# Adaptive sums over the partitions as one 512-column product with ones, columns picked by VectorE, and chunk 2 requested before the rows

## The reference

```python
cond = jax.nn.silu(c)                                   # 1 x 1024
for l in range(DEPTH):                                  # DEPTH = 2
    mod = cond @ ada_w[l] + ada_b[l]                    # ada_w[l]: 1024 x 9216
    sh1, sc1, g1, sh2, sc2, g2, sh3, sc3, g3 = jnp.split(mod, N_MOD, axis=-1)
    hn = _modulate(_rms_norm(h, norm_g[l, 0]), sh1, sc1)
    h = h + 0.5 * g1[:, None, :] * _swiglu(hn, ffn1_w_in[l], ffn1_w_out[l])
    hn = _modulate(_rms_norm(h, norm_g[l, 1]), sh2, sc2)
    h = h + g2[:, None, :] * (mixers(hn @ w_in[l]) @ w_out[l])      # four mixers, in short
    hn = _modulate(_rms_norm(h, norm_g[l, 2]), sh3, sc3)
    h = h + 0.5 * g3[:, None, :] * _swiglu(hn, ffn2_w_in[l], ffn2_w_out[l])
```

## Time and profile before

| | |
|---|---|
| median of 3 runs | 2152.02 us (2151.99 to 2154.15) |
| the profiled execution | 2152.88 us, of which span 2151.1 us |
| TensorE busy | 2051.2 us, 95% |
| VectorE busy | 930.2 us, 43% |
| ScalarE busy | 917.4 us, 43% |
| GpSimd busy | 1332.5 us, 62% |
| mean granted clock of TensorE | 0.974 |

### The profile page before, as it was taken

The page is one execution under the profiler, slowest core; times in us unless marked ns, Lnnn a source line. Parts: engine busy times, 40 slices in busy tenths (PEclk is TensorE's granted clock), DMA queues, the critical chain, the costliest instruction groups (busy, mean ns, idle before and its releaser), DMA issues.

```text
span 2151.1 us, 36602 instructions
## 1 busy us (share of the span) xinstructions
PE 2051.2 (95%) x15510; PEld 1966.5 (91%) x15510; DVE 930.2 (43%) x1761; ACT 917.4 (43%) x1393; POOL 1332.5 (62%) x612
## 2 busy tenths in 40 slices
PE   7999997999989999889999999999999999999998
PEld 4999996899989998769998999989999999988998
DVE  4554776561455477754124422144233432134223
ACT  2443454334444335434444354514544345514543
POOL 1778660477967786217887765505896765405885
PEclk8999998999989999999999999999999999999999
DMA  9997550785689775227555543335554543335552
GB/s 326 357 332 253 186 161 20 254 289 176 195 275 349 244 245 167 79 84 250 177 162 170 170 146 116 103 126 166 186 194 134 192 143 113 118 118 168 185 196 79
DMA packets 356787, 398.18 MB, mean 185 GB/s; under 512 B 8984, under 2 KB 318992, under 8 KB 356624
## 3 DMA queue, kind: packets, MB, share of 16 engines
q1 hardware_dynamic: 356464, 395.65, 55.5%
q10 hardware_dynamic: 160, 0.20, 0.0%
HBM read 394.77 MB, written 1.05 MB: 184 GB/s over the span
## 4 chain that ended last, share of the span: by engine, by line
PE 90%; DVE 5%; ACT 3%; SPq 1%; issue 1%; DMA 1%; DVEq 0%; ACTq 0%
PE bank L706 73%; PE bank L783 5%; PE bank L1108 3%; PE bank L938 1%; PE bank L805 1%; PE bank L900 1%; PE bank L1072 1%; SPq L534 1%; DVE arena L1641 1%; ACT arena L1270 1%; PE bank L697 1%; PE bank L999 1%; DVE arena L1685 1%; DMA arena<-in_ada_w 1%; PE bank L939 1%
## 5 line engine op out<-in xcount | busy, mean ns | idle before, releaser
L672 POOL TENSOR_TENSOR w_lo<-ring,w_hi 128x1024 fp32r<-128x1024 f32 (+2 forms) x608 | 1332.3, 2217 | 798.7 <-ACT w_hi L1169 798.1
L706 PE MATMUL bank<-hn,w_hi 128*128 128x256 f32 x2912 | 848.4, 291 | 26.4 <-DVE hn_lo L1578 15.8
L706 PE MATMUL bank<-hn_lo,w_hi 128*128 128x256 f32 x2912 | 832.4, 286 | 0.0
L706 PE MATMUL bank<-hn,w_lo 128*128 128x256 f32 x2912 | 832.1, 286 | 0.0
L1169 ACT ACTIVATE w_hi<-ring 128x1024 fp32r<-128x1024 f32 (+2 forms) x608 | 576.4, 975 | 485.6 <-PE bank L706 356.8
L706 PEld LDWEIGHTS bank<-hn,w_hi 128*128 128x128 f32 x2912 | 567.6, 195 | 36.7 <-issue 34.6
L706 PEld LDWEIGHTS bank<-hn_lo,w_hi 128*128 128x128 f32 x2912 | 567.8, 195 | 4.5 <-issue 3.8
L706 PEld LDWEIGHTS bank<-hn,w_lo 128*128 128x128 f32 x2912 | 567.3, 195 | 0.0
L706 PE MATMUL bank<-gated,w_hi 128*128 128x256 f32 x1408 | 249.7, 280 | 0.0
L706 PEld LDWEIGHTS bank<-gated,w_hi 128*128 128x128 f32 x1408 | 215.0, 187 | 0.0
L706 PE MATMUL bank<-gated,w_lo 128*128 128x256 f32 x704 | 196.4, 279 | 0.0
(11 more groups left out here) (188 smaller groups left out, 2130.1 us busy)
## 6 DMA issues: line engine op xcount, KB each, us to landing
ring<-in_ffn_w_in SPq DMA_DIRECT2D x88, 1024.0 KB, 6.1
ring<-in_w_in SPq DMA_DIRECT2D x72, 1024.0 KB, 5.1
arena<-in_ada_w SPq DMA_DIRECT2D x35, 2048.0 KB, 10.3
ring<-in_w_up SPq DMA_DIRECT2D x32, 1024.0 KB, 5.4
ring<-in_w_down SPq DMA_DIRECT2D x32, 1024.0 KB, 5.0
ring<-in_ffn_w_out SPq DMA_DIRECT2D x32, 768.0 KB, 4.4
ring<-in_ffn_w_out SPq DMA_DIRECT2D x32, 640.0 KB, 4.0
ring<-in_w_in SPq DMA_DIRECT2D x16, 512.0 KB, 3.6
```

The lines of the kernel that those rows point to most:

```text
L672: pool.tensor_tensor(w_lo[:, q, ks], ring[:, r, k0:k0 + n], w_hi[:, q, ks], ALU.subtract) \
L706: last = mm(out, a, b, start=start and i == 0, stop=stop and i == 2)
```

## The change

1. `ada_reduce` becomes one product: weights are ones (128 x 128), the moving operand is the whole of `ada_acc` (512 columns), the result 128 x 512 in bank 7, the same sums on each partition. From the second one on it first waits until VectorE has taken the columns of the one before it (`ada_taken`).
2. VectorE picks the columns: `take_columns` multiplies 128 x 128 of the bank by the identity and sums each row, four times per chunk, into the new SBUF tile `ada_cols`. `take_sums(n)` does this for all sums up to n that aren't taken yet, after it has waited for their products. `ada_sum` calls it for the sum before its own, `modulation` for all that it needs; `modulation` then adds `ada_cols` instead of PSUM to the bias.
3. Chunks 1 and 3 of layer 0: the product takes one column of `cond` broadcast to 128 weight columns, so its result is on all partitions too; VectorE picks its columns from bank 1. ScalarE's `copy_row` and TensorE's `ada_turn` go. The product of chunk 3 waits until the columns of chunk 1 are taken from bank 1.
4. The request of chunk 2 stands right behind those of chunks 0 and 1, ahead of the rows.

```diff
+ADA_SUMMED = [c for layer in range(L) for c in range(ADA_CHUNKS) if (layer, c) not in ((0, 1), (0, 3))]
...
+        ada_cols = sb("ada_cols", MOD_TILES + 4 * ADA_FIRST)
...
-            for c in range(2):
+            for c in range(3):
                 sp.dma_start(first_ada[c], ada_source(0, c)).then_inc(first_ada_in[c], 16)
...
-            sp.dma_start(first_ada[2], ada_source(0, 2)).then_inc(first_ada_in[2], 16)
...
-                            sp.wait_ge(tensor_done, eng.at("first ada row 3"))
+                            sp.wait_ge(tensor_done, eng.at("first ada 3"))
...
-                n, col = ada_sums(layer, c), ada_column(c)
+                n = ada_sums(layer, c)
                 pe.wait_ge(ada_summed, n + 1)
-                for j in range(4):
-                    js = slice(j * P, (j + 1) * P)
-                    last = mm(bank[:, 7, col + j:col + j + 1], ada_acc[:, n % 2, js], ones[:, 0:1], start=True, stop=True)
-                last.then_inc(ada_reduced, 1)
+                if n:
+                    pe.wait_ge(ada_taken, n)
+                mm(bank[:, 7], ones, ada_acc[:, n % 2], start=True, stop=True).then_inc(ada_reduced, 1)
...
-                        last = mm(bank[0:1, 1, :], cond[:, k:k + 1], first_ada[i][:, j], start=(k == 0), stop=(k == KT - 1))
+                        last = mm(bank[:, 1], cond[:, k:k + 1].to_broadcast([P, P]), first_ada[i][:, j], start=(k == 0),
+                                  stop=(k == KT - 1))
...
-            ada_turn(1)
             ada_reduce(0, 0)
+            pe.wait_ge(vector_done, eng.at("first ada 1 taken"))
             ada_product(3, ((3, 4), (4, 4)))
             ada_reduce(0, 2)
-            ada_turn(3)
...
-            copy_row(1)
             round_chunk("f1in", 0)
-            copy_row(3)
...
+            def take_columns(b, c, done, mark=None):
+                for j in range(4):
+                    js = slice(j * P, (j + 1) * P)
+                    i = dve.tensor_tensor_reduce(out=bank[:, b, js], in0=bank[:, b, js], in1=ident, scale=1.0, scalar=0.0,
+                                                 op0=ALU.mult, op1=ALU.add, accum_out=col(ada_cols, ada_column(c) + j))
+                    if j < 3:
+                        i.then_inc(vector_done, eng.step())
+                    elif done is ada_taken:
+                        i.then_inc(ada_taken, 1)
+                    else:
+                        i.then_inc(vector_done, eng.step(mark))
+
+            taken = [0]
+
+            def take_sums(n):
+                for i in range(taken[0], n + 1):
+                    dve.wait_ge(ada_reduced, i + 1)
+                    dve.sem_inc(passed[1], 1)
+                    take_columns(7, ADA_SUMMED[i], ada_taken)
+                taken[0] = max(taken[0], n + 1)
+
             def ada_sum(layer, c):
+                if ada_sums(layer, c) > 0:
+                    take_sums(ada_sums(layer, c) - 1)
...
                 if summed == (0, 3):
-                    dve.wait_ge(ada_reduced, 2)
                     dve.wait_ge(tensor_done, eng.at("first ada 3"))
+                    take_columns(1, 3, vector_done)
+                    take_sums(1)
                 else:
-                    dve.wait_ge(ada_reduced, ada_sums(*summed) + 1)
+                    take_sums(ada_sums(*summed))
+                dve.wait_ge(vector_done, eng.at())
+                dve.wait_ge(ada_taken, taken[0])
                 at_ = MOD_TILES if first == 0 else first
-                tt(mod[:, first:last], bank[:, 7, at_:at_ + last - first], par_all[:, layer, first:last], ALU.add) \
+                tt(mod[:, first:last], ada_cols[:, at_:at_ + last - first], par_all[:, layer, first:last], ALU.add) \
...
+            dve.wait_ge(tensor_done, eng.at("first ada 1"))
+            take_columns(1, 1, vector_done, "first ada 1 taken")
+            take_sums(0)
             dve.wait_ge(first_ada_in[2], 16)
             partial_sum(1, first_ada[2], bank[:, 3])
```

More of the change, by code:

```diff
@@ L432, in build @@
                      ring[:, 3].rearrange("p (k a) n -> p k (a n)", a=2))
-        ada_row = act_tmp[0:1]
         gated = rounded("gated", 8192, FT, 2, S)
@@ L487, in build @@
         first_ada_in = [sem(f"first_ada_in_{i}") for i in range(5)]
-        ada_summed, ada_reduced = sem("ada_summed"), sem("ada_reduced")
+        ada_summed, ada_reduced, ada_taken = sem("ada_summed"), sem("ada_reduced"), sem("ada_taken")
         x_in, tables_in, rows_in = sem("x_in"), sem("tables_in"), sem("rows_in")
@@ L826, in ada_product @@
                     for j in range(nk):
-                        last = mm(bank[0:1, 1, :], cond[:, k:k + 1], first_ada[i][:, j], start=(k == 0), stop=(k == KT - 1))
+                        last = mm(bank[:, 1], cond[:, k:k + 1].to_broadcast([P, P]), first_ada[i][:, j], start=(k == 0),
+                                  stop=(k == KT - 1))
                         k += 1
-                last.then_inc(tensor_done, eng.step(f"first ada row {c}"))
-            def ada_turn(c):
-                pe.wait_ge(scalar_done, eng.at(f"ada row {c}"))
-                col = ada_column(c)
-                for j in range(4):
-                    last = mm(bank[:, 7, col + j:col + j + 1], ada_row[:, c // 2, j * P:(j + 1) * P], ones[0:1, 0:1],
-                              start=True, stop=True)
                 last.then_inc(tensor_done, eng.step(f"first ada {c}"))
@@ L1297, in attention @@
                     after(i)
-            def copy_row(c):
-                act.wait_ge(tensor_done, eng.at(f"first ada row {c}"))
-                f(ada_row[:, c // 2], bank[0:1, 1, :], ACT.Copy).then_inc(scalar_done, eng.step(f"ada row {c}"))
             norm_root("f1")
-            copy_row(1)
             round_chunk("f1in", 0)
-            copy_row(3)
             for layer in eng.layers("one"):
```

## The result

The changed kernel takes **2160.83 us** (median of 5 runs, 2159.46 to 2162.86), the kernel before 2151.99 in the same comparison (2151.27 to 2154.15). The ratio is 1.004, 95% interval 1.0028 to 1.0052: slower by 8.8 us between the medians, 6 to 11 by the interval. The forecast was 2155.0 with a range of 2148 to 2163, and gave slower by over 0.2% a chance of 0.43, no difference 0.50. The profiled execution took 2160.83 with a span of 2159.0, against 2152.88 and 2151.1: +7.95 us to explain where the prediction had +2.95.

A forecast was written before the change was run, and what follows sets the result against it. TensorE, 90% of the chain, was taken as the bound. Stalls 4.95 and boundaries 0.9, less 0.9 for reductions and 2.0 at the start, gave +2.95 us on 2152.88; less 0.86 for the median, 2155.0, range 2148 to 2163.

The forecast's parts named there:

- likeliest case: Whole kernel: the start's gain and the stalls nearly cancel; 2155 us, own range 2151 to 2160, chance 0.52.
- rival 2: Feed-forward loop: the wait costs more, with no slack anything added counts about 11 times; 2163 us, chance 0.24.
- the loop: f1in and f2in: reduction, picks, sum, multiplication, rounding, GpSimd's split, then TensorE's product of the next pair but one.
- the stall: f1in and f2in: TensorE waits for GpSimd's split at every second pair, 0.3 us each; 2.4 us in f1in.
- the picks: VectorE, between reduction and sum: four picks of 0.21 us, 0.84 in all, plus a 0.13 gap.
- TensorE's own part: Reductions in the matmul stream: one wide product plus the pair's matmuls takes 0.03 us less per sum, -0.9 us in all.
- stalls at each pair: Feed-forward loop: a listed sign of being wrong, since stalls were expected only at every second pair.
- f2in: Second feed-forward's 'in' stage: layer 0 two stalls, 0.6 us, plus 1.65 at pair 5; layer 1 one stall, 0.3.
- The stretched add: Modulation's add, f2in pair 3, layer 0: slowed beside GpSimd's split, +1.5 us for the sum, 1.65 us of stall.
- the boundary: Before norm z: VectorE picks a whole chunk, 0.95 us less slack; +0.7 in layer 0, +0.2 in layer 1.
- the start: Early chunk 2 request: chunk 3 lands 1.0 us earlier, its product regains 1.0 of clock loss; -2.0 us.
- rival 5: Start: the early request brings nothing, since the rows' requests are pushed back by as much; 2157 us, chance 0.08.

The follow-up runs named there:

- e2: The changed kernel with the feed-forward 'in' stages' picks moved from ahead of the pair's sum to behind its last gating; 2153.01 us, 1.0001 to the kernel before.
- e5: The changed kernel with each pick that stands ahead of a sum done twice, the second waiting for the first; 2182.52 us, 1.0142 to the kernel before.
- e4: The kernel before with only the reduction made one 512-column product and nothing that picks, so its modulations are not the reference's; 0.9995 to the kernel before.
- e1: The changed kernel with chunk 2's request back behind the rows; 2160.59 us, 1.0035 to the kernel before.
- e9: The kernel of e2 with the parameter rows requested from ScalarE's queue instead of SyncE's; 0.9994 to the kernel before.
- e12: The changed kernel with picks behind the pair's last gating in the first feed-forwards only, still ahead of the sum in f2in; 2155.53 us, 1.0015 to the kernel before.
- e6: The changed kernel with each adaptive chunk requested only behind the following pair's weights; 2161.3 us, 1.0035 to the kernel before.
- e10: The kernel before with the start of e9 alone (rows requested from ScalarE's queue), four one-column reductions kept; 2151.61 us, 0.9996 to the kernel before.
- e11: The kernel of e10 with layer 1's rows and the norms' rows requested from GpSimd's queue, on their own semaphore; 2147.23 us, 0.9979 to the kernel before.

## Why the prediction was right and wrong

The measured 2160.83 lies in the range, 5.8 us above the number. It is above the likeliest case's own 2151 to 2160 and in the range only because that was drawn up to rival 2 (2163). The loop and its places were right; the sizes were not, and the 2.7 us that come on top in layer 0's mixer had no term at all.

**Right: the loop.** Before any run the prediction named the stall, its place (GpSimd's split, at every second pair), the sum-to-split length to the hundredth (9.04), and the picks (0.84 + 0.13 for 0.96). The last agreement is luck: the picks start 0.25 apart, not 0.21, and the sum follows the fourth without the gap of 0.13. The Trainium skill's 120 cycles for each operation from PSUM (VectorE: DVE Perf Modes, The TRN2 errata) had given an estimated 1.03 for the four; the measured 0.96 lies below it, nearer than the 0.84 of the row. e2 and e5 confirm the loop by taking the wait away and by making it longer. TensorE's own part (-0.9) isn't contradicted by e4, and not shown by it either.

In layer 1 the rhythm is another from the middle of f1in on. Pairs 4 and 6 stall as in layer 0, then the reductions lie 12.64, 12.69 and 12.65 apart: pairs 7 to 10 each lose 0.3, TensorE starting each time just as GpSimd's split lands (begun at 702.53, product at 705.07). The prediction had called stalls at each pair a sign of being wrong; here they are the same loop, with the same loss shared out over twice as many pairs (2.1 us per stage in both layers).

**Mis-sized: a difference of two large numbers.** The stall was 13.45 - 13.18. The release came 0.15 later than copied from the one-column product (1.21 for 1.06) and the split reached TensorE 0.15 later (2.53 for 2.38: I had set the split's end equal to TensorE's start). Of 13.45 that is 2%, of the stall it is all: 0.56 instead of 0.27. For both f1in stages the prediction had 2.4 us, less 0.5 for 16 cheaper reductions. In layer 0 it is 116.81 us from the reduction at 82.96 to that at 199.77, against 114.69 before: 2.1 per stage, 4.2 for 1.9. This is what rival 2 said (a cycle without slack, where whatever is added counts about 11 times), at a price between its and mine. (The table gives layer 1's first feed-forward only +1.1, because its stretch from the norm to the first reduction is 0.7 shorter than before, 39.09 for 39.80.)

**Right size, other parts: f2in.** Predicted 2.25 for layer 0, found 2.5 (stalls of 0.6, 1.5 and 0.6 by the distances of the reductions); 0.3 for layer 1, found 0.3. The stretched add is there:

```profile
459.38 1.18 DVE L1532 TENSOR_TENSOR mod<-ada_cols,arena 128x8 f32<-128x8 f32 x1
...
472.23 0.36 PE L708 MATMUL bank<-hn,w_hi 128*128 128x256 f32 x1 [1.30 <-POOL w_lo L674]
```

1.18 us beside GpSimd's split instead of 0.17, +1.0 where I took +1.5, and TensorE waits 1.30 behind it. The Trainium skill (SBUF — State Buffer, Who interferes with whom) has a second SBUF input share an interface with GpSimd, and the row agrees.

**Mis-sized: the boundary.** Before norm z in layer 0 I took 0.95 of picks less 0.28 of slack. VectorE in the changed kernel:

```profile
252.12 0.42 DVE L1545 TENSOR_TENSOR square<-h 128x256 f32<-128x256 f32 x1
252.76 0.30 DVE L1491 CUSTOM_DVE_ANT_0 bank<-bank,const 128x128 f32<-128x128 f32 x1 [0.21 <-DVE square L1545]
...
253.97 0.17 DVE L1532 TENSOR_TENSOR mod<-ada_cols,arena 128x16 f32<-128x16 f32 x1
```

```profile
257.15 0.55 PE L708 MATMUL bank<-hn,w_hi 128*128 128x256 f32 x1 [3.85 <-DVE hn_lo L1596]
```

From the square's start to the add it is 1.85 us, before it was 0.46 (251.78 to 252.24): 1.39 more, because the picks also wait for the square's end (0.21), which I had left out, and have a gap behind them. TensorE's wait before its next product went from 2.71 to 3.85, +1.14, and this same 3.85 stands in e1, e2, e9 and e12. In layer 1 I had +0.2. From the square's start to that product it is 5.03 us for 4.41, +0.6: the slack of 0.80 that I had read came in part from a slow norm product of TensorE (1.22 us, 0.70 in the changed kernel).

**Not foreseen: the mixer of layer 0.** Its +3.8 us is more than that 1.14. Another 1.7 come between TensorE's first product and 364.5, and 1.0 behind it. In both parts a lower granted clock stands in the windows: 0.57 for 0.85 between 344 and 352 us, 0.58 for 0.89 between 372 and 380. The first of them, the changed kernel and then the kernel before:

```profile
344.00:352.00 8.00, 7.38 (x29) 5.94 (x29) 5.82 (x31) 4.47 (x18) 0.00 (x0) 0.57 0.00 1
```

```profile
344.00:352.00 8.00, 7.43 (x39) 5.71 (x39) 7.36 (x33) 5.21 (x21) 0.00 (x0) 0.85 0.01 3
```

At 0.57 it finished 29 matmuls, at 0.85 there were 39. Kernels that pass through the same code differ here: +3.8 in the changed kernel and e6, +1.9 in e12, +0.9 in e2, +0.1 in e1, -0.3 to +0.2 in those without picks (e4, e10, e11). e12 has the 1.0 behind 364.5 and not the 1.7. What decides which clock an execution gets there stays open, and that the clock is the whole of the 2.7 us isn't shown. The one thing seen to go with it is a small shift in the arrival of the stage; no run isolated it.

Also unexplained: a group of f1out takes 16.53 us, in e2 and e12 as well, where it took 16.44 before and 16.41 in e4, some 0.3 us per layer.

**Mis-sized: the start.** I predicted -2.0 and found -1.56 (first product with the weights at 46.55 instead of 48.11). The queue was read rightly:

```profile
1.24 7.29 SPq L541 DMA_DIRECT2D arena<-in_ada_w  x3
8.56 5.36 SPq L537 DMA_DIRECT2D arena<-in_ada_b  x1
...
26.46 0.32 SPq L537 DMA_DIRECT2D arena<-in_norm_final  x1
27.36 0.58 SPq L609 DMA_DIRECT2D arena<-in_ada_w  x1
```

Chunk 2's own request is through at 8.5; SyncE is held by the one behind it, of `ada_b`, until 13.9 (13.3 predicted), and the rows' requests end at 26.8 (26.0). Chunk 3's first half is asked for at 27.36 (26.5) and takes 7.5 us (7.15); so it lands at about 34.86, where I had 33.65 and before it was 34.65. Its row among the DMA issues (KB each, median us from issue to landing):

```profile
arena<-in_ada_w SPq DMA_DIRECT2D x1, 1024.0 KB, 7.5
```

The early request thus doesn't bring chunk 3 sooner: the DMA engines' idle stretch is only moved, to 22 to 26 us (share 0.39). In this rival 5 (the early request brings nothing) was right. TensorE and VectorE at that place:

```profile
29.53 2.86 PE L699 MATMUL bank<-const,arena 107*128 107x107 f32 x13 [4.05 <-DMA arena<-in_norm_final]
...
33.99 0.14 DVE L1491 DVE_READ_ACCUMULATOR2_ANT ada_cols<- 128x1 f32 x1
...
34.95 3.67 PE L828 MATMUL bank<-arena,cond 128*128 128x512 f32 x8 [0.85 <-DVE ada_cols L1491]
```

TensorE waits 4.05 us for the rows, so that its small work is done only at 34.10. The product of chunk 3 needs two things, the columns of chunk 1 taken and chunk 3 landed, and the profile puts its wait of 0.85 down to VectorE. But chunk 1's last column was read by 34.13; what came at 34.86 is the chunk. In e12, whose code is the same up to here, the profile names it:

```profile
34.88 5.13 PE L828 MATMUL bank<-arena,cond 128*128 128x512 f32 x8 [1.78 <-DMA arena<-in_ada_w]
```

So the step "chunk 3's landing ends last" held, by 0.7 us over the late rows, which I had as a bound (+1). What failed is the 1.0 us that it was to come earlier; none of it came. What was gained is the shorter product alone, 7.1 us instead of 9.25, at a granted clock of 1.00 from 34 to 40 us where it was 0.50 and then 0.60: 2.1 where I had counted 1.0; behind it 0.3 are lost again, where I had set the two picks at nothing. Two errors of about 1 us nearly cancelled, which is luck. e9, e10 and e11, which take the rows off SyncE's queue, start that product 1.7 to 2.7 us sooner.

**The sum.** Predicted +2.95; the profiled execution has +7.95. With the prediction's terms put into the table's stages, the 5.0 between are: 3.1 in layer 0's mixer (3.8 for 0.7), 1.4 up to norm z of layer 0 (+0.3 for -1.1: larger stalls and a smaller gain at the start), 0.6 in layer 1's mixer (0.8 for 0.2), 0.4 in layer 0's second feed-forward, 0.2 in layer 1's first, and -0.9 in the second block, where nothing was changed. Read by term, the larger stalls are some 2.7 of it, the boundaries 0.8, the rest of layer 0's mixer 2.7 and the start 0.4; block 2 and other stretches, none of them isolated, take 1.6 back.

## What to carry over

Where a helper engine's work is moved behind a result of TensorE, write down the whole loop back to TensorE's next need of it and compare it with the period; with no slack, every tenth of a microsecond counts once per loop, so both sums must be kept to tenths and their difference given a range of its own. Here the same work cost next to nothing a few instructions later, where nobody waits behind it. A transfer asked for earlier in an ordered queue pushes back everything else in it: look at what is then late, and consider another engine's queue for the small requests. Where an instruction waits for two things, the profile names one; compare the time of each before you call one the cause.

## Of the hardware, not expected

- **A stall can cost more than its length.** After 0.35 us of waiting the granted clock stayed at 1.00 and the next 96 matmuls took 11.74 us; 1.88 us of waiting (e5) was followed by a clock of 0.50 between 100 and 102 us, and the products took 13.11 us. But 1.30 us at 472.23 was followed by 11.75 us: no loss.
- **A small transfer can be slow while large ones are under way on another queue.** In e9 ScalarE's last row, 4 KB asked for at 18.45, was there only at 28.9, with chunks under way on SyncE's queue; in the changed kernel it was asked for at 26.46 and was there at 29.5. That it stood behind the chunks' data is a guess.
- **A pick over 128 columns** comes every 0.25 us (84.23 to 84.48 from one accumulator read to the next). Its accumulator read takes 0.14 us when it writes to `ada_cols`, where the one in attention took 0.08.
